# Finishing a modulation vector early in a feed-forward stage, and lending its scratch memory to later work

## The reference, cut to what matters

```python
# first layer, end: x = x + down(silu(h @ w_gate) * (h @ w_up)), 2816 hidden features
# second layer
c_act = silu(c)                                        # 1024 values
mod = c_act @ w_mod + b_mod                            # 1024 x 6144 weights, one row of output
sh1, sc1, g1, sh2, sc2, g2 = split(mod, 6)
h = rms(x, norm1_w) * (1 + sc1) + sh1
u, q, k, v = split(h @ w_in)
# state space: a = exp(dt * lam), f = (a - 1) / lam
# bb = f * B ; s[t] = a * s[t-1] + bb u[t] ; y[t] = Re(C s[t]) + d u[t]
x = x + g1 * (mixed @ w_out)
x = x + g2 * conv_ffn(rms(x, norm2_w) * (1 + sc2) + sh2)
```

## Time and profile before

| | before |
|---|---|
| median of 3 runs | 1278.69 us (1277.31 to 1279.43) |
| the profiled execution's own time | 1280.15 us |
| its span in the trace | 1278.4 us |
| TensorE busy | 1228.0 us, 96% of the span |
| VectorE busy | 762.3 us, 60% |
| ScalarE busy | 485.6 us, 38% |
| GpSimd busy | 125.3 us, 10% |
| mean granted TensorE clock | 0.984 of full speed |

### The profile page before, as it was taken

The page is one execution under the profiler, slowest core; times in us unless marked ns, Lnnn a source line. Parts: engine busy times, 40 slices in busy tenths (PEclk is TensorE's granted clock), DMA queues, the critical chain, the costliest instruction groups (busy, mean ns, idle before and its releaser), DMA issues. The chain is left out here.

```text
span 1278.4 us, 15375 instructions
## 1 busy us (share of the span) xinstructions
PE 1228.0 (96%) x6230; PEld 964.9 (75%) x6230; DVE 762.3 (60%) x1224; ACT 485.6 (38%) x738; POOL 125.3 (10%) x124
## 2 busy tenths in 40 slices
PE   7999998899999999999997999879899999999998
PEld 5786665578888788888885785558688878888877
DVE  5536674755665865656555896846755652455542
ACT  5244545734322212222324814564433331333320
POOL 0000000014000800000010930014100000000000
PEclk9999999999999999999998998979899999999999
DMA  9311011222443365554443341102122223222222
GB/s 345 130 62 66 34 66 47 86 100 99 166 153 132 118 206 190 173 173 135 134 154 121 62 88 34 67 6 95 66 99 99 78 73 127 101 99 99 68 91 89
DMA packets 25829, 138.40 MB, mean 108 GB/s; under 512 B 2879, under 2 KB 5152, under 8 KB 16544
## 3 DMA queue, kind: packets, MB, share of 16 engines
q1 hardware_dynamic: 25760, 137.43, 32.0%
HBM read 133.75 MB, written 3.67 MB: 107 GB/s over the span
## 5 line engine op out<-in xcount | busy, mean ns | idle before, releaser
L133 PE MATMUL bank<-xhi_ffn,w_hi_part 128*128 128x512 f32 x704 | 278.1, 395 | 4.4 <-DVE xlo_ffn L233 4.4
L134 PE MATMUL bank<-xlo_ffn,w_hi_part 128*128 128x512 f32 x704 | 277.1, 394 | 0.0
L121 ACT ACTIVATE w_hi_part<-w_raw 128x2048 fp32r<-128x2048 f32 (+1 forms) x96 | 165.8, 1727 | 290.6 <-PE bank L135 288.9
L135 PE MATMUL bank<-xhi_ffn,w_lo_part 128*128 128x512 f32 x704 | 275.2, 391 | 0.0
L127 DVE TENSOR_TENSOR w_lo_part<-w_raw,w_hi_part 128x2048 fp32r<-128x2048 f32 (+1 forms) x96 | 198.4, 2067 | 111.8 <-ACT w_hi_part L121 107.6
L133 PEld LDWEIGHTS bank<-xhi_ffn,w_hi_part 128*128 128x128 f32 x704 | 133.0, 189 | 34.7 <-issue 5.4
L135 PEld LDWEIGHTS bank<-xhi_ffn,w_lo_part 128*128 128x128 f32 x704 | 132.8, 189 | 29.5
L134 PEld LDWEIGHTS bank<-xlo_ffn,w_hi_part 128*128 128x128 f32 x704 | 132.6, 188 | 28.0 <-issue 0.2
L360 DVE SCALAR_TENSOR_TENSOR squares<-bank,param,squares 128x511 f32<-128x511 f32 x88 | 63.9, 747 | 84.7 <-ACT squares L343 83.1
L133 PE MATMUL bank<-hhi,w_hi_part 128*128 128x512 f32 x240 | 94.5, 394 | 1.7 <-DVE hlo L368 1.7
L133 PE MATMUL bank<-hhi_half,w_hi_part 128*128 128x512 f32 x240 | 94.2, 392 | 0.7 <-DVE hlo_half L332 0.7
(11 more groups left out here) (363 smaller groups left out, 1928.5 us busy)
## 6 DMA issues: line engine op xcount, KB each, us to landing
mod_w<-in_w_mod SPq DMA_DIRECT2D x32, 768.0 KB, 4.4
w_raw<-in_w_gu SPq DMA_DIRECT2D x22, 1024.0 KB, 4.8
w_raw<-in_w_down SPq DMA_DIRECT2D x32, 704.0 KB, 4.1
w_raw<-in_w_up SPq DMA_DIRECT2D x22, 1024.0 KB, 4.8
w_raw<-in_w_in_f SPq DMA_DIRECT2D x8, 1024.0 KB, 5.1
w_raw<-in_w_out SPq DMA_DIRECT2D x8, 1024.0 KB, 4.9
w_raw<-in_w_in SPq DMA_DIRECT2D x5, 1024.0 KB, 4.8
x<-in_x SPq DMA_DIRECT2D x8, 256.0 KB, 6.5
```

The costliest lines, as they stand in the source:

```text
L121: act.activation(k.whi[:, slot, 0:width], k.raw[:, slot, 0:width], ACT.Copy).then_inc(k.w_hi, 1)
L133: pe.matmul(out, whi, xhi, start=first, stop=False)
L134: pe.matmul(out, whi, xlo, start=False, stop=False)
L135: return pe.matmul(out, wlo, xhi, start=False, stop=last)
```

## The change

It does four things.

1. The modulation's pace becomes 6 steps in an up turn and 5 in a down turn, so that the 128 steps end in turn 22. Each half chunk of weights is loaded when SyncE is one feed-forward chunk further on.
2. The partitions are summed in groups of four chunks: four matmuls, one into each quarter of bank 7's partitions, with 32 columns of `pick` as weights and 384 columns of `mod_acc` moving. There are four groups, at `turn_of(32 * (m + 1)) + 1`, which is after turns 6, 11, 17 and 23. VectorE then copies the bank to SBUF, TensorE transposes it in three pieces after turn 24, and VectorE adds the bias and makes both scales there. All 16 `reduce` calls of before are gone.
3. The memory that `mod_w` and `mod_acc` held is then free: GpSimd makes `c_lifted` there after turn 24, and ScalarE and VectorE make `cos_sin` in the down turns of the second half (30 to 36), over `xlo_ffn`, with the angles over the place of `xhi_ffn`. The loads of `time` and `ssm_c` move to the feed-forward block.
4. The table load at the block's end goes (the logarithm's table is loaded in turn 35 and kept), and ScalarE rounds weights ahead of the squares in the down turns. Out of the mixing block go all of `turns`, `angle`, `sines`, `cosine`, GpSimd's lift, the rest of the modulation, and the waits on them.

```diff
-    EARLY = 6
-    AT_END = 10
-    UP, DOWN = 4, 3
+    UP, DOWN = 6, 5
+    GROUP = 4
...
+        self.summed_at = self.turn_of(8 * self.N) + 1
...
+    def set_picks(self, dve):
+        dve.memset(self.pick[:, :], 0.0).then_inc(self.picks, 1)
+        dve.wait_ge(self.picks, 1)
+        dve.memset(self.pick[:, 32:33], 1.0).then_inc(self.picks, 1)
...
-                    dve.wait_ge(self.reduced, c - self.KEPT + 1)
+                    dve.wait_ge(self.reduced, (c - self.KEPT) // self.GROUP + 1)
...
-    def reduce(self, pe, c):
-        pe.wait_ge(self.step, 8 * (c + 1))
...
-        for t in range(3):
-            mm = pe.matmul(self.k.bank[7][:, 3 * c + t:3 * c + t + 1], self.acc[:, c % self.KEPT, P * t:P * t + P],
-                           self.k.ones[:, 0:1], start=True, stop=True)
+    def reduce(self, pe, m):
+        pe.wait_ge(self.step, 8 * self.GROUP * (m + 1))
+        for q in range(self.GROUP):
+            mm = pe.matmul(self.k.bank[7][32 * q:32 * q + 32, 0:self.W], self.pick[:, 32 - m:64 - m],
+                           self.acc[:, (self.GROUP * m + q) % self.KEPT, :], start=(m == 0), stop=(m == 3))
         mm.then_inc(self.reduced, 1)
...
-            if turn == (self.turn_of(8 * (c + 1)) + 2 if c < self.EARLY else HALF + KT + 3 + 2 * (c - self.EARLY)):
-                self.reduce(pe, c)
+    def pe_after(self, pe, turn):
+        for m in range(4):
+            if turn == self.turn_of(8 * self.GROUP * (m + 1)) + 1:
+                if m == 0:
+                    pe.wait_ge(self.picks, 2)
+                self.reduce(pe, m)
+        if turn == self.summed_at + 1:
+            pe.wait_ge(self.copied, 1)
+            for t in range(3):
+                mm = pe.transpose(self.k.bank[7][:, P * t:P * t + P], self.acc[:, 0, P * t:P * t + P], self.k.ident)
+            mm.then_inc(self.turned, 1)
+
+    def dve_after(self, dve, chain, turn):
+        if turn == self.summed_at:
+            dve.wait_ge(self.reduced, 4)
+            dve.tensor_copy(self.acc[:, 0, :], self.k.bank[7][:, 0:self.W]).then_inc(self.copied, 1)
+        if turn == self.summed_at + 1:
+            dve.wait_ge(self.turned, 1)
+            chain.link(dve.tensor_tensor(
+                self.mods[:, :].rearrange("p (m q t) -> p m q t", m=4, q=4),
+                self.k.bank[7][:, 0:self.W].rearrange("p (t q r) -> p r q t", t=3, q=4)[:, 0:4, :, :],
+                self.pr("b_mod").rearrange("p (m q t) -> p m q t", m=4, q=4), ALU.add))
...
@@ feed-forward block
-                        if modulation.turn_of(4 * (half - 1)) == n - GU - 4:
+                        if modulation.turn_of(4 * (half - 1)) == n - GU - 3:
                             modulation.load(sp, half)
+                    if n == GU + HALF + KT:
+                        sp.wait_ge(powers_made, 1)
+                        sp.dma_start(ssm_c[:, :, :, :], io["ssm_c"].rearrange("p (a t n) -> p a t n", a=2, t=16))\
+                            .then_inc(c_in, 16)
...
+                pool.wait_ge(c_in, 16)
+                pool.wait_ge(modulation.done, 1)
...
                 for j in range(1, KT - 1):
                     r3.add(pool, k, j)
...
+                        if half == 0 or j < KT - 1:
+                            ffn.act_weights(act, ffn.down_chunk(half, j) + 2)
                         if half == 1:
-                            if j == 0:
-                                act.preload_act_table_set("natural_log_exp_and_others")
                             act.wait_ge(ffn.added, KT + j + 1)
                             r3.act_square(act, k, x[:, j, :], j)
-                        if half == 0 or j < KT - 1:
-                            ffn.act_weights(act, ffn.down_chunk(half, j) + 2)
+                            if j == 0:
+                                act.wait_ge(time_in, 16)
+                                act.wait_ge(col_den, 2)
+                                turns(0)
+                                turns(1)
+                            if j in (1, 2):
+                                turns(j + 1)
+                            if 2 <= j < 6:
+                                sines(j - 2)
+                            if j == 5:
+                                act.preload_act_table_set("natural_log_exp_and_others")
                 r3.act_root(act, KT, eps_col[:, 0:1])
-                act.preload_act_table_set("trig_and_small")
                 ffn.act_weights(act, ffn.down_chunk(1, KT - 1) + 2)
...
+                            if j == 1:
+                                dve.wait_ge(time_in, 16)
+                                dve.wait_ge(a_moved, 2)
+                                dve.tensor_copy(clock, chunk_time).then_inc(time_set, 1)
+                                dve.wait_ge(time_set, 1)
+                            if 1 <= j < 5:
+                                angle(j - 1)
+                            if 3 <= j < 7:
+                                cosine(j - 3)
...
+                pe.wait_ge(angled, 4)
                 r3.pe_sum(pe, k, KT - 2, [KT - 1])
-                for n in range(modulation.AT_END, modulation.N):
-                    modulation.reduce(pe, n)
@@ mixing block
-                sp.wait_ge(time_set, 1)
-                sp.wait_ge(turned, 4)
-                sp.wait_ge(c_taken, 1)
...
-                turns(0)
-                turns(1)
                 act.wait_ge(k.w_used, IN2 + 1)
                 first_tile(IN2, 0, k.bank[0])
```

More of the change, by code:

```diff
@@ new lines, in dve_after @@
+    def dve_after(self, dve, chain, turn):
[8 more added lines that the diff above has]
+                self.pr("b_mod").rearrange("p (m q t) -> p m q t", m=4, q=4), ALU.add))
+            for n, norm in ((1, "norm1"), (4, "norm2")):
+                scale = self.mods[:, 8 * n:8 * n + 8]
+                ins = dve.scalar_tensor_tensor(out=scale, in0=scale, scalar=1.0, in1=self.pr(norm), op0=ALU.add,
+                                               op1=ALU.mult)
+            ins.then_inc(self.done, 1)
@@ L1352, in program @@
         g_ffn = pr("g_ffn")
-        b_in, col_exp, col_sin, col_den, col_inv, a_made, a_turned, a_moved = (
-            k.sem(f"ssm_{w}") for w in ("b_in", "exponents", "sines", "denominator", "inverse", "wide", "turned", "rows"))
+        b_in, col_exp, col_sin, col_den, col_inv, a_made, a_turned, a_moved, powers_made, c_in, lifted = (
+            k.sem(f"ssm_{w}") for w in ("b_in", "exponents", "sines", "denominator", "inverse", "wide", "turned", "rows",
+                                        "powers_made", "c_in", "c_lifted"))
+        time_in, time_set, turned, angled, sined, half_sined, circled = (
+            k.sem(f"circle_{w}") for w in ("time_in", "time_set", "turns", "angles", "sines", "half_sines", "cosines"))
+        time = over("time", [P, S], time_at)
+        angles = over("angles", [P, 4, S], o_at)
+        half_sines = over("half_sines", [P, 2, S], o_at + 4 * TILE)
+        circle = over("cos_sin", [P, 16, 2, NCK], circle_at)
+        lift = over("c_lifted", [P, 2, 16, TS + 1, 32], lift_at)
+        ssm_c = over("ssm_c", [P, 2, 16, 32], rows_at)
+        chunk_time = time[:, :].rearrange("p (c t) -> p c t", t=TS)[:, :, 0]
+        clock = k.bank[6][:, 0:NCK]
         def col(n):
@@ L1523, in _, with turns, sines @@
                 act.preload_act_table_set("silu_and_others")
+                def turns(b):
+                    ang = angles[:, b, :]
+                    for q in range(4):
+                        mark = chain.mark(act.activation(
+                            ang[:, NCK * q:NCK * q + NCK], chunk_time, ACT.Identity, bias=round_cols[:, 0:1],
+                            scale=col(TURN)[:, 4 * b + q:4 * b + q + 1]))
+                    chain.need(mark)
+                    act.activation(ang, ang, ACT.Identity, bias=round_cols[:, 1:2]).then_inc(turned, 1)
+                def sines(b):
+                    ang, half_sine = angles[:, b, :], half_sines[:, b % 2, :]
+                    act.wait_ge(angled, b + 1)
+                    act.activation(circle[:, 4 * b:4 * b + 4, 1, :], ang.rearrange("p (t c) -> p t c", c=NCK), ACT.Sin,
+                                   scale=6.283185).then_inc(sined, 1)
+                    if b >= 2:
+                        act.wait_ge(circled, b - 1)
+                    chain.link(act.activation(half_sine, ang, ACT.Sin, scale=3.1415925))
+                    act.activation(half_sine, half_sine, ACT.Square).then_inc(half_sined, 1)
                 for half in range(2):
@@ L1647, in _, with angle, cosine @@
                 dve.wait_ge(r2.inverted, 1)
+                def angle(b):
+                    ang = angles[:, b, :]
+                    dve.wait_ge(turned, b + 1)
+                    for part, op in ((TH_HI, ALU.subtract), (TH_LO, ALU.add)):
+                        for q in range(4):
+                            a = ang[:, NCK * q:NCK * q + NCK]
+                            mark = chain.mark(dve.scalar_tensor_tensor(
```

(21 more changed lines are left out.)

149 lines of the change are left out of this document (37 added, 112 removed).

## The result

The changed kernel took **1291.38 us** in the median, its runs from 1283.05 to 1296.36, against 1277.94 us (1275.30 to 1279.43) for the kernel before on the same chip. The ratio is 1.0093, 95% interval 1.0069 to 1.0117. So it is slower, as predicted, but above the range of 1279.5 to 1289.5, and its runs lie over 13 us where those of the kernel before lie over 4. One more execution, of 2446.62 us, is of another, slow state; it counts in the median, which is 1290.87 without it, and not in the range and the ratio. The profiled execution took 1296.36 us, span 1294.5, 16.1 us more than the span before.

The account below looks back on a forecast made before the run. TensorE, busy 96% of the span, was taken to bound the kernel. Terms +3.1 +5.0 +1.5 -1.5 -1.3 -0.5 gave +6.3 us, hence a median of 1285.0 us, range 1279.5 to 1289.5.

Parts of the forecast that it names:

- Turn 9's lateness: Feed-forward turn 9: six multiplies instead of four, all slowed against GpSimd, delay turn 11's hidden tile; +3.1 us.
- The wait at the block sum: After turn 11: TensorE waits for steps 61 to 64 before the second group's sum; +5.0 us, bounds 1.7 to 5.5.
- The clock: Around turn 11's two waits: 3.1 us of TensorE work at half speed; +1.5 us, bounds 0 and twice that.
- The sums: Feed-forward turns: nine reductions go (-5.9), four block sums and three transposes come (+4.4); -1.5 us.
- The rival on the other side: Turn 11: no stall beyond program order, sums worth -2.2 us; total -2.3 us, 1276.4 us; chance 0.10.
- Together: Feed-forward: the lateness, block-sum wait, clock and sums terms together, +8.1 us.
- The second half and the barrier: Second-half turns: lift and table-making cost 0; feed-forward's end barrier: ScalarE's table load goes, -1.3 us.
- The first tile: Mixing block's start: TensorE no longer waits for ScalarE's first tile copy behind two `turns`; -0.5 us.
- The mixing block's rest: Mixing block: the other removed work lay under a full TensorE; 0 us.
- a longer cold spell in turn 11: Rival of a longer cold spell or late weight transfer: 2 to 4 us more, 1287 to 1289; within the forecast's 0.75.

Follow-up runs that it names:

- the second kernel: The kernel before plus 32 single-column filler matmuls on TensorE behind its last feed-forward norm sum; 1283.26 us, ratio 1.0039.

## Why the prediction was right and wrong

- **Turn 9's lateness** (+3.1): the multiplies took 1.6 us as read from the earlier trace rows, and the tile came 3.6 us later in its turn. TensorE, which also arrived 0.7 us sooner, waited 5.02 against 0.65. So +4.4, a size off by 1.3.
- **The wait at the block sum** (+5.0, bounds 1.7 to 5.5): 3.63. The steps were done 5.3 us after the tile, where the sum had 5.8: three slow, one quick. And TensorE's work between the two waits took 1.65 us (442.24 to 443.89) at the lower clock, not 0.8, which shortened the wait and belongs to the next term. Right place, size off by 1.4.
- **The clock** (+1.5, bounds 0 to 3): half speed from 441 to 451 us, 2.5 us. The 3.1 us of cold work was read from one restart; here two waits with a bit of work between them kept it down for 5.1 us of work.
- **The sums** (-1.5): a block sum takes 1.11 us from the matmul ahead of it to the one behind, less the ordinary 0.23, or 0.9; in turns, 1.0 (turn 6 to turn 7: 396.67 - 384.59 = 12.08 against 11.09). The transposes take 0.33. These sizes are as predicted. But all ten reductions of the turns count, not nine: without the one after turn 9 TensorE arrives 0.7 us sooner, which is in the 5.02 above. That makes 6.6 less 3.9 to 4.3, or -2.3 to -2.7. With the stall taken out the same ten count, and the old wait of 0.65 goes as well: without GpSimd's powers the feed-forward is 3.4 us shorter than before the change, 0.65 and 2.7. The rival on the other side had 2.2 for the sums in that case.
- **Together**: 4.4 + 3.6 + 2.5 of stall, less the 2.7, is the +7.8 measured in the feed-forward, against +8.1. The mechanism was right; that the total came within 0.3 is luck, since the errors of its parts cancelled.
- **The second half and the barrier**: no wait of TensorE for `angles`, `cos_sin` or the lift (GpSimd's last lift began at 622.35); -1.45 at the barrier against -1.3.
- **The first tile** (-0.5): the wait of 0.49 is gone, but from the restart to `v2` only 0.16 us is won (39.42 against 39.58). The rest went to the clock: after the restart it was at half for 4.1 us (699.49 to 703.62) where it had been for 3.1, which is up to 0.5 us. The stretch to `v2` follows this time in the other profiles without the wait: 39.1 us where the clock was back after 3.6 us, 40.0 where it was after 5.4. The prediction had no such difference.
- **The mixing block's rest** (0): this is the step that failed. "The rest of what is removed lay under a full TensorE: 0" and the count of the sums by their time alone left out what 61 missing matmuls do to where the instruction blocks begin. `v2` cost **+10.1 us** in the profiled execution, and the late block 5 to 6.5 in the median. With the borders moved by half a block, or with the narrow write gone, the same change gives 1286.2 and 1284.9, beside a forecast of 1285.0; neither of those kernels is the one that was to be predicted. The range had no case for it: I took its upper side from a longer cold spell in turn 11, and the cold spell came 300 us later.
- The feed-forward began 1.4 us sooner than before; in the experiments it began anywhere from 317.9 to 321.4 us, so that is chance. The last 1.2 us, between `inputs` and the end (534.7 against 533.5), lie within the 530.9 to 535.1 of all profiles.

What stays open is why the fetch waits so long behind the write. The runs show that the narrow write and the position of the borders are both needed for the spread, and that the late packet comes while the write is still running, not after it. They do not show what sets the bad place apart: blocks at other places, and once at the bad one, came in time during the same write. By which of its 16 engines a block comes, and what queues ahead of it, no view shows, and it was not tested with writes of other widths. Only three profiles are of a kernel that spreads, two stalled and one not, so how late the block is in the executions between is not known.

## What to carry to other kernels

Removing instructions is not only worth their time: it moves everything behind them against the borders of the engine's instruction blocks. If a kernel's runs spread suddenly after a harmless edit, look for an "issue" wait in the middle of independent matmuls, for the last instruction packet ahead of it, and for a long transfer from few partitions in between; try to write such data from all partitions. That cured the changed kernel and gained nothing in the kernel before, whose blocks came in time. Filler of half a block is a cheap test that tells this cause from the others.

A step that shares its time with GpSimd has to be priced at the slow rate, and so has everything that VectorE does behind it: thinning it out by a third only moved the wait; thinning it to what VectorE's own slack holds removed it.

## What the runs showed of the hardware

- A transfer of 1536 KB took 33 us from 8 partitions (128 copies of each) and 10.3 us from 128 (8 copies of each).
- TensorE's instruction packets of 16 KB were 38 us apart around that narrow write, where they are 22 us apart without it, and TensorE stood 3.55 us (3.09 in the second kernel) with no wait in its program. In three other profiles blocks came in time during such a write. From 706.3 us to the stop it had executed 270 matmuls and 270 weight loads.
- After that gap the granted clock was at its lower level from 744.5 to 765 us with TensorE busy all the time; at turn 11 it was back 3.5 us after the last wait. A short gap can so cost more than a long one: 3.55 us idle, 6.5 us more lost behind it in `v2`.
- VectorE's step with two SBUF inputs takes 0.617 us alone and 1.55 to 1.6 us against GpSimd. The Trainium skill, SBUF — State Buffer, section Who interferes with whom, says that only the port pair which VectorE shares with GpSimd causes contention, and that an instruction of VectorE with two SBUF inputs contends with one of GpSimd that reads SBUF; the trace agrees in that the 128x512 operations that read PSUM keep their 0.68 us (L320) while the ones with two SBUF inputs (L328) take 1.78.
